# First modulation by halves of its columns, and the first four tiles multiplied meanwhile

## What is computed

```python
c_act = jax.nn.silu(c)                                   # c: (1, 1024)
mod = c_act @ ada_w[0] + ada_b[0]                        # ada_w[0]: (1024, 6 * 1024)
sh1, sc1, g1, sh2, sc2, g2 = jnp.split(mod, 6, axis=-1)
hmix = rmsnorm(x, norm_mix[0]) * (1.0 + sc1) + sh1       # x: (512, 1024)
proj = hmix @ w_in                                       # w_in: (1024, 4096): q, f_pre, i_in, g
```

## Time and profile before

| | us |
|---|---|
| median of 3 runs | 2373.59 |
| lowest and highest | 2371.36, 2373.80 |
| the profiled execution | 2373.22 |
| its span, from the first to the last instruction | 2371.9 |
| TensorE's granted clock over the span | 0.996 of 2.4 GHz |

### The profile page before, as it was taken

The page is one execution under the profiler, slowest core; times in us unless marked ns, Lnnn a source line. Parts: engine busy times, 40 slices in busy tenths (PEclk is TensorE's granted clock), DMA queues, the critical chain, the costliest instruction groups (busy, mean ns, idle before and its releaser), DMA issues.

```text
span 2371.9 us, 27771 instructions
## 1 busy us (share of the span) xinstructions
PE 2333.3 (98%) x11065; PEld 1894.9 (80%) x11065; DVE 1204.3 (51%) x1865; ACT 878.3 (37%) x1362; POOL 481.6 (20%) x536
## 2 busy tenths in 40 slices
PE   8999999999999999999999999999999999999999
PEld 6888877888787877777888888888887868888887
DVE  6545755555424446626545336444335974444423
ACT  4322245454223448833233234233225353333321
POOL 0102833545002038810000010000011870000000
PEclk9999999999999999999999999999999999999999
DMA  8664035666223310022333233332332212333322
GB/s 295 195 194 143 2 95 164 190 190 187 98 91 111 91 56 1 1 63 88 99 98 95 93 97 98 98 96 91 100 103 91 81 36 78 92 97 98 98 97 81
DMA packets 169335, 247.43 MB, mean 104 GB/s; under 512 B 14889, under 2 KB 110694, under 8 KB 169206
## 3 DMA queue, kind: packets, MB, share of 16 engines
q1 hardware_dynamic: 156276, 200.93, 26.6%
q0 software_dynamic: 12624, 44.54, 6.2%
q10 hardware_dynamic: 306, 0.19, 0.0%
HBM read 243.51 MB, written 2.10 MB: 104 GB/s over the span
## 4 chain that ended last, share of the span: by engine, by line
PE 88%; DVE 6%; POOL 2%; ACT 1%; issue 1%; DMA 0%; SPq 0%; DVEq 0%; ACTq 0%; POOLq 0%
PE ps L582 79%; DVE dsa_mask L2504 1%; PE ps L1021 1%; DVE w_lo L1923 1%; PE ps L719 1%; POOL nsa_p L2845 1%; PE ps L1037 1%; DVE small L2502 1%; PE ps L554 1%; DVE h_lo L2020 1%; PE ps L1011 0%; PE ps L1010 0%; POOL hg_k L2747 0%; PE ps L1251 0%; DVE hg_scT L2138 0%
## 5 line engine op out<-in xcount | busy, mean ns | idle before, releaser
L1923 DVE TENSOR_TENSOR w_lo<-w_raw,w_hi 128x1024 fp32r<-128x1024 f32 (+2 forms) x358 | 443.4, 1239 | 1007.1 <-ACT w_hi L1339 1006.8
L1339 ACT ACTIVATE w_hi<-w_raw 128x1024 fp32r<-128x1024 f32 (+2 forms) x364 | 380.7, 1046 | 1088.4 <-PE ps L582 1088.3
L582 PE MATMUL ps<-h_hi,w_hi 128*128 128x512 f32 (+1 forms) x1928 | 757.0, 393 | 4.9 <-DVE w_lo L1923 3.3
L582 PE MATMUL ps<-h_hi,w_lo 128*128 128x512 f32 (+1 forms) x1928 | 750.6, 389 | 0.0
L582 PE MATMUL ps<-h_lo,w_hi 128*128 128x512 f32 (+1 forms) x1928 | 750.4, 389 | 0.0
L582 PEld LDWEIGHTS ps<-h_hi,w_hi 128*128 128x128 f32 (+1 forms) x1928 | 361.3, 187 | 93.8 <-issue 7.6
L582 PEld LDWEIGHTS ps<-h_hi,w_lo 128*128 128x128 f32 (+1 forms) x1928 | 361.3, 187 | 76.8
L582 PEld LDWEIGHTS ps<-h_lo,w_hi 128*128 128x128 f32 (+1 forms) x1928 | 361.4, 187 | 75.7 <-issue 1.7
L582 PE MATMUL ps<-hid_hi,w_hi 128*128 128x512 f32 x616 | 240.9, 391 | 0.0
L582 PE MATMUL ps<-hid_lo,w_hi 128*128 128x512 f32 x616 | 239.7, 389 | 0.0
L582 PE MATMUL ps<-hid_hi,w_lo 128*128 128x512 f32 x616 | 239.7, 389 | 0.0
(11 more groups left out here) (389 smaller groups left out, 2605.6 us busy)
## 6 DMA issues: line engine op xcount, KB each, us to landing
w_raw<-in_ffn_w_up SPq DMA_DIRECT2D x264, 256.0 KB, 3.1
w_raw<-in_ffn_w_down SPq DMA_DIRECT2D x176, 256.0 KB, 2.8
m_raw<-in_ada_w POOLq DMA_DIRECT2D x80, 512.0 KB, 4.5
w_raw<-in_ffn_w_gate SPq DMA_DIRECT2D x88, 256.0 KB, 2.8
w_raw<-in_hg_w_in SPq DMA_DIRECT2D x64, 256.0 KB, 3.1
w_raw<-in_nsa_w_in SPq DMA_DIRECT2D x40, 256.0 KB, 2.9
w_raw<-in_w_in SPq DMA_DIRECT2D x32, 256.0 KB, 2.8
m_acc<-in_ada_w SPq DMA_DIRECT2D x9, 512.0 KB, 6.0
```

The source lines that it names most:

```text
L582: ins = K.nc.tensor.matmul(out, lhsT, rhs, start=start, stop=stop)
L1339: K.nc.scalar.activation(K.half(K.w_hi[u % SPL], width), K.half(K.w_raw[u % RAW], width), ACT.Copy) \
L1923: K.nc.vector.tensor_tensor(K.half(K.w_lo[u % SPL], width), K.half(K.w_raw[u % RAW], width), hi, ALU.subtract) \
```

## The change

1. Each of the 16 modulation loads now brings, for one tile of 128 rows, 512 columns of the shift and the same 512 of the scale. Units 0 to 7 are the columns of output tiles 0 to 3 (half 0), units 8 to 15 those of tiles 4 to 7 (half 1).
2. SyncE loads weight unit 0 behind modulation unit 4 (was behind 12) and weight unit 1 behind unit 8 (was behind 15).
3. TensorE sums the squares of tiles 0 to 3 ahead of the small transposes, then those of tiles 4 to 7, then the columns of half 0; 4 matmuls without use follow (there were 12 and 5).
4. VectorE awaits half 0 behind unit 8 (`vector_first_mod`), splits weight unit 1 behind unit 12, and after half 1 makes scalings and low parts for tiles 4 to 7 only.
5. GpSimd splits weight unit 0 (high and low), and makes `xT * rstd` and the low parts of tiles 0 to 3. ScalarE makes the scaled and shifted tile in place and copies it to `h_hi` (two instructions a tile).
6. TensorE multiplies the first group tile by tile (`tensor_first_group`), with the columns of half 1 ahead of tile 3.
7. GpSimd's loads wait for half 1 (`first_added`, 1) and stand behind its new work.

```diff
@@ sync_program
+        both = lambda ap: ap.rearrange("p (a c) -> p a c", a=2)
+        half = slice(u // KD * 512, u // KD * 512 + 512)
+        nc.sync.dma_start(both(K.first[u % FIRST]), both(K.io["ada_w"][0, u % KD * P:(u % KD + 1) * P, 0:2 * D])[:, :, half]) \
             .then_inc(*K.first_landed[u % FIRST].up(u, 16))
-        if u == 2 * KD - 4:
+        if u == 4:
             weights(0)
-    for u in range(1, len(K.units)):
+        elif u == KD:
+            weights(1)
+    for u in range(2, len(K.units)):
         weights(u)
@@ tensor_start
-    pe.wait_ge(*K.rows_landed.at("all"))
-    for tile in range(1, len(K.vec_rows)):
-        turn_rows(tile)
     pe.wait_ge(*K["x_in"].at(KD - 1))
-    tensor_norm_rest(K, "first", 0)
+    for kt in range(KD):
+        if kt == 4:
+            pe.wait_ge(*K.rows_landed.at("all"))
+            for tile in range(1, len(K.vec_rows)):
+                turn_rows(tile)
+        tensor_square_sum(K, "first", kt)
+    tensor_first_columns(K, 0)
     pe.wait_ge(*K["vec_copied"].at(3))
-    for part in range(2):
-        pe.wait_ge(*K["mod_ready"].at(("first", 8 * part + 7)))
-        tensor_mod_columns(K, (0, part), part, 4 + part)
-        tensor_stay_busy(K, 12 if part == 0 else 5, 7)
+    tensor_stay_busy(K, 4, 7)
+def tensor_first_group(K, u0, banks):
+    for kt in range(KD):
+        u, c0 = u0 + kt // 2, kt % 2 * 512
+        hi, lo = K.w_hi[u % SPL], K.w_lo[u % SPL]
+        if kt == 3:
+            tensor_first_columns(K, 1)
+        K.pe.wait_ge(*K["h_high"].at(("hg_in", kt)))
+        if kt % 2 == 0:
+            K.pe.wait_ge(*w_low(K, u))
...
+        K.pe.wait_ge(*h_low(K, "hg_in", kt))
...
@@ scalar_start
-    scalar_split(K, 0)
-    scalar_norm_apply(K, "first", "hg_in", lambda kt: K.mod[:, 0, 0, kt:kt + 1], "ms01")
+    scalar_split(K, 1)
+    nt = K.scratch["first"][1]
+    act.wait_ge(*K["mod_ready"].at(("first_scaled", 0)))
+    for kt in range(KD):
+        t, shift = nt[kt % 4][:, :], K.mod[:, 0, 0, kt:kt + 1]
+        if kt < 4:
+            act.wait_ge(*K["normed_pool"].at(kt))
+            nc.scalar.activation(t, t, ACT.Identity, bias=shift, scale=K.mod[:, 0, 1, kt:kt + 1]).then_inc(*K["small_act"].up(("feature", kt)))
+            act.wait_ge(*K["small_act"].at(("feature", kt)))
+            nc.scalar.activation(K.h_hi[:, kt, :], t, ACT.Copy).then_inc(*K["h_high"].up(("hg_in", kt)))
+        else:
+            act.wait_ge(*K["scaled"].at(("first", kt)))
+            nc.scalar.activation(K.h_hi[:, kt, :], t, ACT.Identity, bias=shift).then_inc(*K["h_high"].up(("hg_in", kt)))
@@ vector_start, in the loop over the 16 units and behind it
+        elif u == KD:
+            vector_first_mod(K, 0)
         elif u == KD + 4:
-            vector_mod_add(K, 0, 0, 4)
-    vector_split(K, 0)
-    vector_mod_add(K, 0, 1, 5)
-    vector_scales(K, 0, 1, "norm_mix")
-    vector_norm_apply(K, "first", "hg_in", lambda kt: K.mod[:, 0, 1, kt:kt + 1], lambda kt: K.mod[:, 0, 0, kt:kt + 1], "ms01")
+            vector_split(K, 1)
+    vector_first_mod(K, 1)
...
+    for kt in range(4, KD):
+        dve.wait_ge(*h_low(K, "hg_in", kt - 4))
+        nc.vector.scalar_tensor_tensor(nt[kt % 4][:, :], K.xT[:, kt, :], K.mod[:, 0, 1, kt:kt + 1], rstd[:, :], ALU.mult, ALU.mult) \
+            .then_inc(*K["scaled"].up(("first", kt)))
+        if kt > 4:
+            low(kt - 1)
+    low(KD - 1)
@@ gpsimd_program
-    K.pool.wait_ge(*K["mod_ready"].at("mod01"))
+    gpsimd_first_features(K)
+    K.pool.wait_ge(*K["mod_ready"].at(("first_added", 1)))
+def gpsimd_first_features(K):
...
+    pool.wait_ge(*K.raw_landed[0].at(0))
+    nc.gpsimd.tensor_copy(K.w_hi[0][:, :], K.w_raw[0][:, :]).then_inc(*K["normed_pool"].up("w_high"))
+    pool.wait_ge(*K["normed_pool"].at("w_high"))
+    nc.gpsimd.tensor_tensor(K.w_lo[0][:, :], K.w_raw[0][:, :], K.w_hi[0][:, :].bitcast(F32), ALU.subtract).then_inc(*K["w_low_pool"].up(0))
+    pool.wait_ge(*K["rstd"].at("first"))
+    def normed(kt):
+        pool.wait_ge(*K["x_in"].at(kt))
+        nc.gpsimd.tensor_tensor(nt[kt][:, :], K.xT[:, kt, :], rstd[:, :], ALU.mult).then_inc(*K["normed_pool"].up(kt))
+    def low(kt):
+        pool.wait_ge(*K["h_high"].at(("hg_in", kt)))
+        nc.gpsimd.tensor_tensor(K.h_lo[:, kt, :], nt[kt][:, :], K.h_hi[:, kt, :].bitcast(F32), ALU.subtract) \
+            .then_inc(*K["h_low_pool"].up(("hg_in", kt)))
+    normed(0)
+    normed(1)
+    low(0)
+    normed(2)
+    low(1)
+    normed(3)
+    low(2)
+    low(3)
```

More of the change, by code:

```diff
@@ L404, in w_low, with h_low @@
 def w_low(K, u):
-    return K["w_low_pool" if u - K.unit["dsa", 0] in DSA_LOW_BY_POOL else "w_low"].at(u)
+    return K["w_low_pool" if u == 0 or u - K.unit["dsa", 0] in DSA_LOW_BY_POOL else "w_low"].at(u)
+def h_low(K, h_tag, kt):
+    return K["h_low_pool" if h_tag == "hg_in" and kt < 4 else "h_low"].at((h_tag, kt))
 def norm_order(tag):
@@ L672, in tensor_hgrn_in @@
                 elif gi:
-                    pe.wait_ge(*K["mod_ready"].at("mod01"))
+                    pe.wait_ge(*K["mod_ready"].at(("first_added", 1)))
             if i == 0 and gi == 0:
                 pe.wait_ge(*K["rstd"].at(("first", "ln")))
-            tensor_group(K, "hg_in", K.unit["hg", n, gi], range(4 * gi, 4 * gi + 4), 512 if n == "v" else None,
-                         first=n == "f" and gi == 0)
+                tensor_first_group(K, K.unit["hg", n, gi], range(4))
+                continue
+            tensor_group(K, "hg_in", K.unit["hg", n, gi], range(4 * gi, 4 * gi + 4), 512 if n == "v" else None)
 def evac_wait(K, e, key):
@@ L1960, in vector_scales, with vector_first_mod @@
         .then_inc(*K["mod_ready"].up(f"ms{layer}{part}"))
+def vector_first_mod(K, half):
+    cols = slice(4 * half, 4 * half + 4)
+    K.dve.wait_ge(*K["mod_summed"].at(("first", half)))
+    K.nc.vector.tensor_tensor(K.mod[:, 0, 0:2, cols], K.ps[:, 4 + half, 0:KD].rearrange("p (a k) -> p a k", a=2), K.mod_b[:, 0, 0:2, cols],
+                              ALU.add).then_inc(*K["mod_ready"].up(("first_added", half)))
+    K.dve.wait_ge(*K["mod_ready"].at(("first_added", half)))
+    K.nc.vector.scalar_tensor_tensor(K.mod[:, 0, 1, cols], K.mod[:, 0, 1, cols], 1.0, K.v["norm_mix"][:, cols], ALU.add, ALU.mult) \
+        .then_inc(*K["mod_ready"].up(("first_scaled", half)))
 def vector_start(K):
@@ L1982, in vector_start @@
     for u in range(2 * KD):
-        part, kt, slot = u // KD, u % KD, u % FIRST
-        acc, c = K.m_acc[:, part, :], K.cvec[:, kt:kt + 1]
+        half, kt, slot = u // KD, u % KD, u % FIRST
+        acc, c = K.m_acc[:, half, :], K.cvec[:, kt:kt + 1]
         dve.wait_ge(*K.first_landed[slot].at(u))
@@ L1994, in vector_start @@
                 keep_rows(tile)
+        elif u == KD:
+            vector_first_mod(K, 0)
         elif u == KD + 4:
-            vector_mod_add(K, 0, 0, 4)
-    vector_split(K, 0)
-    vector_mod_add(K, 0, 1, 5)
-    vector_scales(K, 0, 1, "norm_mix")
-    vector_norm_apply(K, "first", "hg_in", lambda kt: K.mod[:, 0, 1, kt:kt + 1], lambda kt: K.mod[:, 0, 0, kt:kt + 1], "ms01")
+            vector_split(K, 1)
+    vector_first_mod(K, 1)
+    nt, rstd = K.scratch["first"][1:]
+    dve.wait_ge(*K["rstd"].at("first"))
+    def low(kt):
+        dve.wait_ge(*K["h_high"].at(("hg_in", kt)))
+        nc.vector.scalar_tensor_tensor(K.h_lo[:, kt, :], nt[kt % 4][:, :], K.mod[:, 0, 0, kt:kt + 1], K.h_hi[:, kt, :].bitcast(F32),
+                                       ALU.add, ALU.subtract).then_inc(*K["h_low"].up(("hg_in", kt)))
+    dve.wait_ge(*K["mod_ready"].at(("first_scaled", 1)))
+    for kt in range(4, KD):
[5 more added lines that the diff above has]
+    low(KD - 1)
     dve.wait_ge(*K["small_act"].at("lb"))
@@ L2680, in gpsimd_program, with low @@
     gpsimd_plain_squares(K, "dsa")
+def gpsimd_first_features(K):
+    nc, pool, (_, nt, rstd) = K.nc, K.pool, K.scratch["first"]
+    pool.wait_ge(*K.raw_landed[0].at(0))
[6 more added lines that the diff above has]
+        nc.gpsimd.tensor_tensor(nt[kt][:, :], K.xT[:, kt, :], rstd[:, :], ALU.mult).then_inc(*K["normed_pool"].up(kt))
+    def low(kt):
+        pool.wait_ge(*K["h_high"].at(("hg_in", kt)))
[9 more added lines that the diff above has]
+    low(3)
 def gpsimd_squares(K, tag):
```

17 lines of the change are left out of this document (14 added, 3 removed).

## The result

The changed kernel takes 2378.43 us (median of 13 runs, 2377.21 to 2381.24); the kernel before, run beside it, 2371.46 us (13 runs, 2369.89 to 2375.49). The ratio is 1.0028, with an interval of 1.0021 to 1.0036: slower by 7.0 us or 0.28%. The forecast was 2380.8 us, range 2374.5 to 2384.5. The profiled execution took 2377.47 us for a span of 2376.2.

What follows compares the result with a forecast made beforehand. TensorE, busy 98%, was taken as the bound, its unbroken run starting at unit 2 (50.07 us) after VectorE's start-up work. Base 2373.22, plus 5.9 for unit 2's later start, plus 1.7 for half clock: 2380.8 us, range 2374.5 to 2384.5.

Steps and rivals of the forecast that it cites:

- Two engines at one resource: VectorE's units 9 to 14 and unit 1's split alternate with GpSimd's instructions: seven pairs of 2.22 us, unit 15 ending 45.5.
- Unit 2's split behind all of it: On VectorE the split stands behind tiles 4 to 7, so early tiles 0 to 3 bring nothing; unit 2 starts at 56.0.
- The chain behind unit 15: Column sums and tiny instructions 2.6 us, 0.1 to the next, tiles 4 to 7 5.9, then 1.9 to TensorE on unit 2.
- The loads: Half loads cost 0 to 0.8 us; reordering delays those behind by about 1.25, unit 5 to about 19.3, at no cost.
- GpSimd's modulation load: First load moves from 38.70 to about 51 us, just in time for use at 55.9; hidden.
- The clock at the sums of squares: Half clock on TensorE behind a 1.3 us gap: sums end at 25.7 us, 24.3 if the clock does not fall.
- The stall at unit 8: VectorE, behind unit 8, waits for the half-0 columns until 27.5 us: a stall of some 2.5 us.
- The clock on the columns of half 1 and on tile 3: No half clock taken here: columns and two tiny instructions 2.6 us, tile 3 done near 50.5, TensorE then idle 5.5.
- The clock behind unit 2: After TensorE's idle gap ahead of unit 2, 3.4 us run at half clock: +1.7 us, ends 0 and 3.4.
- No sharing: Rival: VectorE and GpSimd do not take turns; unit 2 starts at 49.2 us, total 2374.0, no change; chance 0.12.
- Sharing with a warm clock in one of the two places: Rival: full clock at the sums or behind unit 2, 2379.1 or 2379.4 us; chance 0.24 for one or both places.

Runs made afterwards that it cites:

- run 1: Changed kernel with GpSimd's eight scalings and low parts of tiles 0 to 3 acting on 8 of 512 columns: 2373.45 us, ratio 1.0003 to the kernel before.
- run 2: Changed kernel with modulation units 8 to 14 accumulating in PSUM, unit 15 writing the sum to SBUF: 2371.97 us, ratio 0.9997 to the kernel before.
- run 3: Changed kernel with unit 2's split moved behind tile 3 on ScalarE and behind unit 15 on VectorE: 2373.06 us, ratio 1.0006 to the kernel before.
- run 4: Changed kernel with busy matmuls ahead of tile 2, the half-1 columns and tile 4: 2375.89 us, ratio 1.0014 to the kernel before.
- run 8: Changed kernel with VectorE making tiles 0 to 3's scalings and low parts, and unit 2's split moved up: 2369.95 us, ratio 0.9989 to the kernel before.

## Why the prediction was right

*Two engines at one resource* carried the sum, and it held: 27.42 to 43.21 us for seven pairs is 2.26 us a pair, where 2.22 had been read off one collision 300 us away in another stage. GpSimd's own time beside VectorE was 2.25, as forecast. Runs 1 and 2 show it to be the cause: with GpSimd's work gone, or with one VectorE input in PSUM, unit 15 ends 7.3 and 6.1 us sooner, and the ratio is back at 1.0003 and 0.9997.

*Unit 2's split behind all of it* was named as the reason why early tiles bring nothing at the end. TensorE's 3.04 us idle ahead of unit 2, released by that split, and run 3, which moves it, show it. The chain behind unit 15 was as worked out: 5.8 us for tiles 4 to 7 (5.9) and 1.9 from there to TensorE (1.9).

*The loads* delayed unit 5 to 19.27 us (19.3 forecast), and that was hidden. One meeting of the two engines is not in the sum at all: GpSimd's low part of weight unit 0 was still under way when VectorE came to unit 5, and held it up, so that units 5 and 6 took 3.81 us, where two of them take 2.67.

```profile
18.25 2.36 POOL L2765 TENSOR_TENSOR w_lo<-w_raw,w_hi 128x1024 fp32r<-128x1024 f32 x1
...
19.27 3.81 DVE L2050 SCALAR_TENSOR_TENSOR m_acc<-m_raw,cvec,m_acc 128x1024 f32<-128x1024 f32 x2 [2.00 <-DMA m_raw<-in_ada_w]
```

These 1.1 us were hidden here too, since the sums of squares on TensorE ended only then (24.64); in runs 3, 4 and 8, where the sums ended sooner, TensorE waited for unit 7. GpSimd's modulation load, moved behind everything, landed in time: VectorE used it at 55.37 without a wait.

*Wrong terms, which offset one another:*
- The clock at the sums of squares. I took half clock behind a gap of 1.3 us; the gap was 1.34 and the sums ran at full clock: 24.64 us instead of 25.7, although they began at 16.90 and not at 16.3.
- The stall at unit 8: 0.93 us instead of 2.5. About 1.1 us of the difference is the clock; the rest is that unit 8 itself ended at 25.58, not 25 (without the 1.1 us of the meeting at unit 5 it would have been 24.5).
- The clock on the columns of half 1 and on tile 3. I had both at full clock; they ran at half (columns 2.87 us for 1.8, tile 3 to 52.55 us instead of 50.5). From the end of unit 15 to the scaling of tile 4 it took 3.4 us instead of 2.7: 0.7 on the path. The second cost nothing, because TensorE then had to wait for unit 2 anyway: so the idle time was 3.04 us and not 5.5.
- The clock behind unit 2 fell as forecast: 0.51 from 55.67 to 59.08, 1.6 us.

Minus 1.2 at unit 9, plus 0.3 for the slower pairs, plus 0.7 at the columns and minus 0.1 for tiles 4 to 7 make minus 0.3 to 0.4: +5.5 at unit 2 where +5.9 was forecast, and +7.1 at unit 4 against 5.9 + 1.7 = 7.6. That the two errors on the clock have opposite signs is luck; without the second the forecast for unit 2 would have been 1.1 us off. The rest of the distance between 2380.8 and 2378.43 is the base: the sum was made against 2373.22, and the kernel before had its median at 2371.46 beside the changed one.

The rivals were priced well. *No sharing* (2374.0, no change) is what run 1 built: 2373.45. *Sharing with a warm clock in one of the two places* gives 2379.4 with the sums warm and unit 2 cold, which is what the trace shows; the forecast and this rival differ only in that term. It leaves out the half clock on the columns, though, which no rival had. What had a name but no price was the way out: nothing in the prediction asked what the same change would do with its accumulator in PSUM or with the split moved, and together they turn a loss of 0.28% into a gain of 0.30%.

## What to carry to other kernels

Before work is handed to GpSimd beside a busy VectorE, count how many VectorE instructions of that stretch read two inputs from SBUF: here each pair cost 2.26 us where VectorE alone needed 1.39, and doing both jobs on VectorE needed 1.86. With the accumulator in PSUM the units were back at 1.39 beside GpSimd's work; leaving the work with VectorE cost 1.86, less than GpSimd's help. And a consumer that starts sooner gains nothing while its next input is produced behind everything else in a queue: move that first, then measure.
